# The front of a two-block transformer kernel: value tile channel by token, triangles as 32-column diagonal blocks

## The reference, cut to what matters

```python
h = modulate(rmsnorm(x, norm1_g), shift1, scale1)
hc = modulate(rmsnorm(xc, norm1_g), modc[0], modc[1])            # 256 context tokens
q, k, v, rw, gl = jnp.split(h @ w_in, IN_SPLITS, axis=-1)
qc, kc, vc, rwc, glc = jnp.split(hc @ w_in, IN_SPLITS, axis=-1)
...
ya = latent_window_attention(q, k, v, kc, vc, sink)              # 8 query heads, 2 key/value heads of 64
r_l, v_l, hg_l, kk_l, dirs_l = rwkv_prepare(short_conv(rw, conv_w), ...)   # and the same for the context

# the recurrence that the prepared tensors feed, in both directions, 8 heads of 64
def step(S, inp):
    r_t, w_t, kk_t, b_t, k_t, v_t = inp
    sa = jnp.einsum('bhvk,bhk->bhv', S, -kk_t)
    S = S * w_t[:, :, None, :] + sa[..., None] * b_t[:, :, None, :] + v_t[..., None] * k_t[:, :, None, :]
    y = jnp.einsum('bhvk,bhk->bhv', S, r_t)
```

## Time and profile before

| | us |
|---|---|
| median of 3 runs | 3498.15 (3492.49 to 3511.63) |
| the profiled execution, its own time | 3513.24 |
| its span | 3511.4 |
| TensorE busy | 3171.9 (90%) |
| VectorE busy | 1919.5 (55%) |
| ScalarE busy | 1167.7 (33%) |
| GpSimd busy | 1566.5 (45%) |

### The profile page before, as it was taken

The page is one execution under the profiler, slowest core; times in us unless marked ns, Lnnn a source line. Parts: engine busy times, 40 slices in busy tenths (PEclk is TensorE's granted clock), DMA queues, the critical chain, the costliest instruction groups (busy, mean ns, idle before and its releaser), DMA issues. The chain is left out here.

```text
span 3511.4 us, 47020 instructions
## 1 busy us (share of the span) xinstructions
PE 3171.9 (90%) x18292; PEld 2493.9 (71%) x18292; DVE 1919.5 (55%) x2784; ACT 1167.7 (33%) x2305; POOL 1566.5 (45%) x1195
## 2 busy tenths in 40 slices
PE   5898999999789999799999999999897999899796
PEld 2666787788578888567788878887674666676574
DVE  3278754646434455777633463347314887666736
ACT  4145433223334443422211121102223664245713
POOL 1114646364234441466666666666450002555342
PEclk9989869999889999899999999999996999999888
DMA  4235545322144442542333333334434221222111
GB/s 169 77 120 150 162 131 174 100 79 85 57 121 136 133 134 62 170 125 88 93 96 96 96 90 96 96 102 117 127 109 116 61 61 58 78 83 66 42 55 72
DMA packets 524177, 358.50 MB, mean 102 GB/s; under 512 B 92481, under 2 KB 477238, under 8 KB 523958
## 3 DMA queue, kind: packets, MB, share of 16 engines
q1 hardware_dynamic: 513302, 325.09, 31.9%
q0 software_dynamic: 4608, 16.78, 1.6%
q10 hardware_dynamic: 6048, 13.63, 1.1%
HBM read 276.72 MB, written 78.18 MB: 101 GB/s over the span
## 5 line engine op out<-in xcount | busy, mean ns | idle before, releaser
L2438 PE MATMUL psum<-place,place 128*128 128x512 f32 x2126 | 861.2, 405 | 82.8 <-POOL place L2416 33.4
L2439 PE MATMUL psum<-place,place 128*128 128x512 f32 x2126 | 841.3, 396 | 0.0
L2440 PE MATMUL psum<-place,place 128*128 128x512 f32 x2126 | 839.6, 395 | 0.0
L2414 POOL CAST place<-place 128x1024 fp32r<-128x1024 f32 (+3 forms) x302 | 306.2, 1014 | 1097.8 <-PE psum L2440 658.1
L2416 POOL TENSOR_TENSOR place<-place,place 128x1024 fp32r<-128x1024 f32 (+3 forms) x302 | 693.7, 2297 | 24.1
L2438 PEld LDWEIGHTS psum<-place,place 128*128 128x128 f32 x2126 | 408.0, 192 | 200.9 <-POOL place L2416 51.9
L2439 PEld LDWEIGHTS psum<-place,place 128*128 128x128 f32 x2126 | 407.6, 192 | 90.1 <-issue 7.8
L2440 PEld LDWEIGHTS psum<-place,place 128*128 128x128 f32 x2126 | 407.0, 191 | 87.3
L657 PE MATMUL psum<-place,place 128*128 128x512 f32 (+1 forms) x712 | 289.2, 406 | 21.8 <-issue 10.3
L658 PE MATMUL psum<-place,place 128*128 128x512 f32 (+1 forms) x712 | 274.4, 385 | 0.0
L659 PE MATMUL psum<-place,place 128*128 128x512 f32 (+1 forms) x712 | 274.0, 385 | 0.0
(11 more groups left out here) (327 smaller groups left out, 5369.9 us busy)
## 6 DMA issues: line engine op xcount, KB each, us to landing
place<-in_w_mlp_up SPq DMA_DIRECT2D x64, 512.0 KB, 4.0
place<-in_w_mlp_down SPq DMA_DIRECT2D x64, 512.0 KB, 3.6
place<-in_w_out SPq DMA_DIRECT2D x48, 512.0 KB, 3.6
chunked<-place SPq DMA_DIRECT2D x64, 320.0 KB, 3.6
place<-in_w_in SPq DMA_DIRECT2D x34, 512.0 KB, 5.6
solve<-in_w_ada POOLq DMA_DIRECT2D x32, 512.0 KB, 6.1
place<-in_lru_w_in SPq DMA_DIRECT2D x32, 512.0 KB, 4.0
place<-in_mla_w_in SPq DMA_DIRECT2D x30, 512.0 KB, 4.1
```

What stands on the lines that cost most here:

```text
L2414: nc.gpsimd.tensor_copy(hi, raw).then_inc(self.w_split, 1)
L2438: pe.matmul(ps, self.w_hi[:, j, k, :], hi, start=(k == 0), stop=False)
L2439: pe.matmul(ps, self.w_hi[:, j, k, :], lo, start=False, stop=False)
L2440: mm = pe.matmul(ps, self.w_lo[:, j, k, :], hi, start=False, stop=(k == kt - 1))
```

## The change

1. The value tile is computed as the other tiles: weights stationary, tokens moving, result channel by token; it is stored as it is (`vt` is 128 x 1280). `Window` loads it as it is to `v_raw` (in the place of the later `out` and beyond; `mask` moves ahead of it), transposes ten 128 x 128 blocks on TensorE in WIN slots 3, 4 and 5 to banks 6 and 7, and ScalarE copies them to `v`. The first turn of probabilities waits for the three copies.
2. The triangles: instead of 20 products of 128 x 128 an item, 80 products of 32 x 32, the diagonal blocks alone, each at its own 32 PSUM partitions (k), the head half e in bank 2 + e. All 40 of one direction stand in one slot, o = 13 for direction 0 and o = 15 for direction 1, and ScalarE copies them with one instruction of 2 x 160 columns on 128 partitions, at o = 14 and 16. SP's store is at o = 17 and its report at o = 19. An item has 20 offsets for 21.
3. `load` in PREP waits on SP until the store of the tile that it reads has landed.

```diff
-    LEAD, PER, DEPTH, BLOCKS = 2, 8, 21, 4 * 20
+    LEAD, PER, DEPTH, BLOCKS = 2, 8, 20, 4 * 20
...
-              10: ["e10", "e20", "e30", "e11", "e21", "e31"], 13: ["d0"], 14: ["d1"], 15: ["d2", "d3"], 16: ["d4"],
-              17: ["d5"]}
-    ON_PE = {2: ["z0"], 4: ["z1"], 5: ["kkc"], 6: ["a0"], 7: ["spread"], 8: ["a1"], 11: ["bon"], 12: ["n0"], 13: ["n1"], 14: ["n2", "n3"], 15: ["n4"],
-             16: ["n5"]}
-    TRIANGLES = [(m % 2, 4 * (m // 2), (4, 4, 2)[m // 2]) for m in range(6)]
+              10: ["e10", "e20", "e30", "e11", "e21", "e31"], 14: ["d0"], 16: ["d1"]}
+    ON_PE = {2: ["z0"], 4: ["z1"], 5: ["kkc"], 6: ["a0"], 7: ["spread"], 8: ["a1"], 11: ["bon"], 13: ["n0"], 15: ["n1"]}
...
         def load(n, x):
             if n >= 1:
                 sp.wait_ge(self.dstep, self.last_conv(n - 1, x))
+            sp.wait_ge(self.stored, 16 * (3 * (n // 2) + 3 + "krv".index(x)))
...
-                        act.wait_ge(self.pstep, pv[n - 1, "n5" if d else "n3"])
+                        act.wait_ge(self.pstep, pv[n - 1, f"n{d}"])
...
-                elif 13 <= o <= 17:
-                    for name in self.ON_ACT[o]:
-                        m = int(name[1])
-                        e, u0, nu = self.TRIANGLES[m]
-                        act.wait_ge(self.pstep, pv[n, f"n{m}"])
-                        if n >= 1 and m == 0:
-                            act.wait_ge(self.diag_out, 16 * n)
-                        ps = C.psum[:, 2 + m % 2, 0:nu * CH].rearrange("p (u c) -> p u c", c=CH)
-                        for k in range(CH // BK):
-                            r = slice(BK * k, BK * (k + 1))
-                            a = nc.scalar.activation(self.diag[r, 10 * e + u0:10 * e + u0 + nu, :], ps[r, :, r],
-                                                     ACT.Copy)
-                        a.then_inc(self.astep, 1)
+                elif o in (14, 16):
+                    d = (o - 14) // 2
+                    act.wait_ge(self.pstep, pv[n, f"n{d}"])
+                    if n >= 1 and d == 0:
+                        act.wait_ge(self.diag_out, 16 * n)
+                    nc.scalar.activation(self.diag.rearrange("p (e d u) c -> p e d (u c)", e=2, d=2)[:, :, d, :],
+                                         C.psum[:, 2:4, 5 * BK * d:5 * BK * (d + 1)], ACT.Copy).then_inc(self.astep, 1)
...
-                        for x in range(nu):
-                            d, c = (u0 + x) // 5, (u0 + x) % 5
-                            A, B = (self.results(d)[y][64 * e:64 * e + 64, c * CH:(c + 1) * CH] for y in (0, 2))
-                            mm = pe.matmul(C.psum[:, 2 + m % 2, x * CH:(x + 1) * CH], A if d else B, B if d else A,
-                                           start=True, stop=True)
-                        mm.then_inc(self.pstep, 1)
+                elif o in (13, 15):
+                    d = (o - 13) // 2
+                    if d:
+                        pe.wait_ge(self.astep, ac[n, "d0"])
+                    elif n >= 1:
+                        pe.wait_ge(self.astep, ac[n - 1, "d1"])
+                    pe.wait_ge(self.dstep, dv[n, f"B{d}"])
+                    for c in range(5):
+                        for k in range(CH // BK):
+                            for e in range(2):
+                                at = slice(c * CH + BK * k, c * CH + BK * (k + 1))
+                                A, B = (self.results(d)[y][64 * e:64 * e + 64, at] for y in (0, 2))
+                                mm = pe.matmul(C.psum[BK * k:BK * (k + 1), 2 + e, BK * (5 * d + c):BK * (5 * d + c + 1)],
+                                               A if d else B, B if d else A, start=True, stop=True)
+                    mm.then_inc(self.pstep, 1)
...
+        self.v_parts = {3: (0, 4), 4: (4, 4), 5: (8, 2)}
...
-        sp.dma_start(self.v, self.vt.rearrange("(t p) n -> p t n", p=P)).then_inc(self.loaded, 16)
+        sp.dma_start(self.v_raw, self.vt).then_inc(self.loaded, 16)
...
+                    for x in range(count):
+                        mm = pe.transpose(C.psum[:, 6 + (s - 3) % 2, x * P:(x + 1) * P],
+                                          self.v_raw[:, (first + x) * P:(first + x + 1) * P], C.mat("ident"))
+                    mm.then_inc(self.v_turned, 1)
...
+            if u == 0:
+                pe.wait_ge(self.v_copied, 3)
...
+                nc.scalar.activation(self.v[:, first:first + count, :],
+                                     C.psum[:, 6 + (s - 3) % 2, 0:count * P].rearrange("p (t n) -> p t n", n=P),
+                                     ACT.Copy).then_inc(self.v_copied, 1)
...
-                  column(C_V, [(a, n, a) for a, n in chunks(ALL)], token_rows, by_token=True)]
+                  column(C_V, [(a, n, a) for a, n in chunks(ALL)], lambda st: [(vt, st[:, 0:ALL])])]
```

More of the change, by code:

```diff
@@ L817, in sync @@
                     sp.dma_start(self.bonus[q * P:(q + 1) * P, t:t + m], self.out[:, a:a + m]).then_inc(self.b_out, 16)
-                elif o == 18:
-                    sp.wait_ge(self.astep, at["act"][n, "d5"])
+                elif o == 17:
+                    sp.wait_ge(self.astep, at["act"][n, "d1"])
                     sp.dma_start(self.blocks[self.BLOCKS * n:self.BLOCKS * (n + 1), :, :]
                                  .rearrange("(u k) r c -> (k r) u c", k=CH // BK), self.diag).then_inc(self.diag_out, 16)
-                elif o == 20:
+                elif o == 19:
                     sp.wait_ge(self.diag_out, 16 * (n + 1))
@@ L1183, in __init__ @@
         self.z = C.slot(0, 2, 512, at=at_t)
+        self.mask = tile(2, P)
+        at_out = place[0]
         self.out = tile(2, NQ // 2, P)
-        self.mask = tile(2, P)
-        self.end = place[0]
+        self.v_raw = C.slot(0, 1, ALL, at=at_out)[:, 0, :]
+        self.end = max(place[0], at_out + ALL)
+        assert self.end <= SLOTS * SLOT - 2 * KD * 256
+        self.v_parts = {3: (0, 4), 4: (4, 4), 5: (8, 2)}
         self.UNITS = (T // P) * (NQ // 2)
@@ L1199, in __init__ @@
         self.out_sent = C.pair("out_sent")
+        self.v_turned, self.v_copied = C.sem("v_turned"), C.sem("v_copied")
     def blocks(self, u):
@@ L1279, in tensor @@
                         .then_inc(self.rot, 1)
+                if s in self.v_parts:
+                    first, count = self.v_parts[s]
+                    if s == 3:
+                        pe.wait_ge(self.mem_h, 4)
+                        pe.wait_ge(self.mem_l, 4)
+                    elif s == 5:
+                        pe.wait_ge(self.v_copied, 1)
+                    for x in range(count):
+                        mm = pe.transpose(C.psum[:, 6 + (s - 3) % 2, x * P:(x + 1) * P],
+                                          self.v_raw[:, (first + x) * P:(first + x + 1) * P], C.mat("ident"))
+                    mm.then_inc(self.v_turned, 1)
             yield
@@ L1352, in scalar @@
                         .then_inc(self.mem_h, 1)
+            elif s in self.v_parts:
+                first, count = self.v_parts[s]
+                act.wait_ge(self.v_turned, s - 2)
+                nc.scalar.activation(self.v[:, first:first + count, :],
+                                     C.psum[:, 6 + (s - 3) % 2, 0:count * P].rearrange("p (t n) -> p t n", n=P),
+                                     ACT.Copy).then_inc(self.v_copied, 1)
             yield
@@ L1468, in front @@
     lin.memory = win.mem_hi, win.mem_l
+    prep.stored = lin.stored
     LIN, PREP, WIN, SOLVE = range(4)
@@ L3757, in block_kernel @@
         kraw = C.scratch("kraw", P, WP)
-        vt = C.scratch("vt", ALL, P)
+        vt = C.scratch("vt", P, ALL)
         rw = C.scratch("rw", 3 * RW + DL + IL + GL, WP)
@@ L3788, in padded @@
             return lambda st: [(dst[r0:r0 + n, :], st[0:n, :])]
-        def token_rows(st):
-            return [(vt.rearrange("(t p) n -> p t n", p=P), st[:, 0:ALL].rearrange("p (t n) -> p t n", n=P))]
         def lat_rows(dst, r0):
```

## The result

The changed kernel takes 3464.49 us in the median of 4 runs (3458.36 to 3469.89), the kernel before 3504.89 in 4 runs (3492.49 to 3518.91): ratio 0.9884, 95% interval 0.9851 to 0.9918. The difference of the medians is 40.4 us, the forecast's sum. That it fits to a tenth is luck: two steps were off by more than 10 us and cancelled, as the two traces show. Of the kernels tried later, late_both had one run of 3956.79 us at a granted clock of 0.732, against 3430 to 3452 us in its five others; its ratio and median leave that run out.

The account below looks back on a forecast made before the run. TensorE was taken as the bound, alone from 460 to 580 us and nearly tied with VectorE from 200 to 460. Terms -27.8 - 3 - 7 - 8 + 4 + 1.4 = -40.4 us gave 3458 from the median; range 3428 to 3489.

Parts of the forecast that it names:

- The value tile, -27.8: Front: 128-column matmuls become 512 and 256 columns at full clock, 41.7 to 13.9 us, saving 27.8 us of TensorE time.
- The neighbours' clock, -3: TensorE work beside the value tile returns from half to full clock: 5.1 us possible, 3 taken.
- The price of one instruction of a small product: Triangles in the front: 10.5 ns from a 32x32 row, doubled to 21; 3.4 us an item, 14 us saved in all.
- Half of it counted: Of the triangles' 14 us, 7 counted, since about half falls where VectorE sets the pace (200 to 460 us).
- -8 for the later place: Triangles one slot later in the front shorten TensorE's waits by 12 us, less 4 us lost to VectorE at the value tile.
- The waits ahead of the triangles: TensorE's waits for VectorE there summed to 29.5 us; the gain lay between 0 and -27, -12 taken.
- The waits move to the bonus product: With TensorE early, VectorE would be found waited for at slot 11's bonus product or the later triangles.
- new waits above 20 us: Sign of being wrong: TensorE's new waits for VectorE at L1032 or for GpSimd at L657 above 20 us.
- GpSimd, +4: Front: with a shorter value tile, weight splits of the last query and first gate tiles come just as wanted; +4 us (0 to 8).
- ScalarE's copies, the new wait in `load`, the window: Fewer, wider triangle copies: 0; the load's wait for stores: 0; ten window transposes: +1.4 us on TensorE.
- reach the end whole: After 600 us the rest was taken as a TensorE chain, so the front's gain would pass undiminished to the end.
- Rival C: Triangles in the front: 32-column blocks don't overlap, 103 ns each, +91 us against -33 elsewhere, about 3556 us; chance 0.07.

Follow-up runs that it names:

- late_both: Changed kernel plus 434 TensorE waits at the recurrence's start, preparation from weight slot 13 instead of 15, front solver slots after every second weight slot: 0.9805, median 3433.08 us.
- v_only: Kernel before with only the value tile's edits (tile, store, load, transposes), triangles as before: ratio 0.9936 against the kernel before.
- tri_only: Changed kernel with the value tile, its store and load as before, so only the triangles' edits: ratio 1.0043 against the kernel before.
- tri_early: Changed kernel with the triangles one slot earlier (TensorE at 12 and 14, ScalarE at 13 and 15): ratio 0.9894 against the kernel before.
- tri_x4: Changed kernel with each 32x32 triangle product issued four times to the same place: ratio 1.0083 against the kernel before.
- the last three kernels: Changed kernel with 434 waits at the recurrence's start, plus preparation from slot 13, thinner solver slots, or both: 0.9847, 0.9849, 0.9805 against the kernel before.

## Why the prediction was right, and where it was not

- The value tile, -27.8: right. In v_only the tile took 14.5 us, a saving of 27.2, and the front is 27.4 us shorter with everything counted; in the changed kernel the tile itself took 16.9 us, since its first piece began at half clock, a saving of 24.8. That VectorE would follow was right too: the 17.1 us wait of the earlier trace rows is gone and no new one of that size stands there.
- The neighbours' clock, -3: right in kind (0.91 against 0.72 over 460 to 550 us); not measured by itself.
- The price of one instruction of a small product, 21 ns taken between 10.5 and 103: it was 10.3, the lower bound. The doubling for 8 places instead of 16 was the mis-sized term. By the 60 cycles that the Trainium skill gives a matmul (TensorEngine Tiling (Array Packing), Instruction Overhead) it would have been 25, an estimate from the page; the row decides. TensorE's busy time for triangles fell by 33.8 us, not by 14.
- Half of it counted, because VectorE sets the pace, and -8 for the later place: this step failed. The two together were forecast at -15 and are -31.3 in tri_only's front. The place alone is about -10 of them (tri_early). VectorE was busy 215.7 of 260 us, and I read that as a bound. It had 44 us of idle time, and in the changed kernel it works 243.0 of the same 260. A near tie in busy time is not a tie in pace. I take it that much of each engine's idle time was made by its place behind the other: one slot of place gave 10 us of front (tri_early), and of 119 us added to TensorE 70 were paid (tri_x4).
- The waits ahead of the triangles, taken at 29.5 us in 8: a misreading. The 6.2 us of weight loads in the earlier trace rows are the same wait as one of the seven that make 23.3 us (both end at 219.31 us), so the bound of -27, between which and 0 the -12 was chosen, was nearer -21.
- The waits move to the bonus product: right, 23.4 us at L1024 against 9.4 before, the longest 9.0. The prediction named new waits above 20 us there as a sign of being wrong; 14.0 are new.
- GpSimd, +4: right in kind; it is 12.3 us of waits, in the last query tiles. It isn't all lost, since TensorE would have waited for VectorE in part of them.
- ScalarE's copies, the new wait in `load`, the window: no cost seen. The window is 1.7 us shorter, not 1.4 longer, less than it moves by with the same window code (343.7 and 352.1 us). A kernel without the new wait in `load` wasn't tried, as it is not free of races.
- Missing altogether: +15.2 us in the recurrence. The forecast let what the front gained "reach the end whole". 13.1 of it are seven gaps in which TensorE had no instructions, each ended by a packet's landing; the change moved the recurrence in the stream by 1575 instructions. Rival C's sign would have come out through it: with the triangles alone, each of them cheap, the kernel is slower by 0.43%.

So -56.7 stands against -41.8 forecast for the front, and +15.2 against nothing.

Open in part: tri_early and tri_x4 stand at the same place modulo 256 as the changed kernel, and their recurrences are 11.4 and 7.2 us shorter. The gaps say why: 5.7 and 7.8 us of idle time in "issue" against 13.1, in one profile each. So the place alone doesn't fix the loss. What makes a packet late in one chunk of the recurrence and not in the next stays open, and so does why the last three kernels, at 0, take 440 to 444 us: 4.6 to 6.7 us of that are such gaps again.

## What to carry to other kernels

Price a small matmul by a row of the same tile shape where the trace has one, and take its floor seriously if neighbours go to different parts of the array. An engine busy 83% of a stretch need not be its bound; look at who waits for whom. When an edit changes the number of instructions of an engine, compare later stages that nobody edited: if idle time there has no releaser, see whether it ends just after a packet of the instruction queue, and shift the stream by some instructions before you judge the edit.

## What the runs showed of the hardware that was not expected

TensorE's instructions arrive in packets of 16 KB, 256 instructions. In a stage of many small matmuls beside heavy loads, 97 instructions more in front of it cost 40 us of 430 (the kernel before, 429.7 to 470.1 us). 29.7 of them are gaps with no releaser in the profile, the longest 5.2 us, and the long ones end 1.3 to 1.6 us after a packet has landed. Instructions made of two reached waits follow each other at 106 ns; 217 of them left TensorE idle for 18.1 us at the start of the window and 38.6 at the start of the recurrence, where 20.3 are waiting for a load in any case. Instructions of 64x32 products of 32 columns cost 10.3 ns each at changing places and 21 ns when four products in a row go to one place. The granted clock fell to 1.2 GHz in the 128-column value tile at 475 us while TensorE had no idle time. In v_only the same tile, begun at the same time and at full clock, held it with 512 and 256 columns. Wide pieces don't prevent every drop: in the changed kernel the tile began at half clock.
